# Three seven-product units per chunk of the gate and up projections, in place of two, with the sums of weights and the closing sums reordered

## What is computed

```python
def swiglu(x, w_gate, w_up, w_down):
    return (jax.nn.silu(x @ w_gate) * (x @ w_up)) @ w_down
h = h + 0.5 * swiglu(rms_norm(h, ffn1_norm[l]), ffn1_w_gate[l], ffn1_w_up[l], ffn1_w_down[l])
```

## Time and profile before

| | before |
|---|---|
| time, median of 3 runs | 1835.81 us |
| profiled execution: first to last instruction | 1834.2 us |
| PE busy | 99% |
| DVE busy | 82% |
| ACT busy | 54% |
| DMA | 380.36 MB, mean 207 GB/s |
| mean granted TensorE clock | 0.999 |

### The profile page before, as it was taken

The page is one execution under the profiler, slowest core; times in us unless marked ns, Lnnn a source line. Parts: engine busy times, 40 slices in busy tenths (PEclk is TensorE's granted clock), DMA queues, the critical chain, the costliest instruction groups (busy, mean ns, idle before and its releaser), DMA issues. The chain is left out here.

```text
span 1834.2 us, 29749 instructions
## 1 busy us (share of the span) xinstructions
PE 1819.6 (99%) x10696; PEld 1546.4 (84%) x10696; DVE 1505.4 (82%) x1755; ACT 995.2 (54%) x1181; POOL 11.1 (1%) x23
## 2 busy tenths in 40 slices
PE   9999999999999999999999999999999999999998
PEld 7888888888888888999998878888888888888886
DVE  5888888888988985788867866688888888889996
ACT  7555555545555655754535655545555555555554
POOL 1000000000000000000000000000000000000000
PEclk9999999999999999999999999999999999999999
DMA  7677666777766778564443557677777677676664
GB/s 252 221 219 228 219 216 215 220 229 236 233 202 204 225 224 267 173 184 140 138 116 106 176 171 261 180 232 231 229 224 232 216 227 222 217 240 195 209 208 157
DMA packets 207851, 380.36 MB, mean 207 GB/s; under 512 B 16016, under 2 KB 35728, under 8 KB 207504
## 3 DMA queue, kind: packets, MB, share of 16 engines
q1 hardware_dynamic: 206768, 377.08, 65.7%
q10 hardware_dynamic: 480, 1.97, 0.3%
q0 software_dynamic: 512, 0.06, 0.0%
HBM read 360.19 MB, written 18.87 MB: 207 GB/s over the span
## 5 line engine op out<-in xcount | busy, mean ns | idle before, releaser
L402 ACT CAST whi<-raw 128x1024 fp32r<-128x1024 f32 (+1 forms) x648 | 675.1, 1047 | 700.8 <-DVE raw L1476 189.6
L411 DVE TENSOR_TENSOR wlo<-raw,whi 128x1024 fp32r<-128x1024 f32 (+1 forms) x648 | 771.7, 1212 | 208.4 <-ACT whi L402 194.5
L428 PE MATMUL psA<-whi,xh 128*128 128x512 f32 (+1 forms) x572 | 219.5, 384 | 0.5 <-DVE wlo L411 0.5
L428 PE MATMUL psA<-whi,xl 128*128 128x512 f32 (+1 forms) x572 | 219.2, 383 | 0.0
L428 PE MATMUL psA<-wlo,xh 128*128 128x512 f32 (+1 forms) x572 | 219.1, 383 | 0.0
L428 PE MATMUL psB<-whi,xh 128*128 128x512 f32 x544 | 211.7, 389 | 0.0
L428 PE MATMUL psB<-wlo,xh 128*128 128x512 f32 x544 | 211.6, 389 | 0.0
L428 PE MATMUL psB<-whi,xl 128*128 128x512 f32 x544 | 211.6, 389 | 0.0
L428 PEld LDWEIGHTS psA<-whi,xh 128*128 128x128 f32 x572 | 107.4, 188 | 21.6 <-DVE wlo L411 0.7
L428 PEld LDWEIGHTS psA<-whi,xl 128*128 128x128 f32 x572 | 107.4, 188 | 21.2
L428 PEld LDWEIGHTS psA<-wlo,xh 128*128 128x128 f32 x572 | 107.4, 188 | 21.0
(11 more groups left out here) (520 smaller groups left out, 3447.3 us busy)
## 6 DMA issues: line engine op xcount, KB each, us to landing
raw<-in_ffn_w_gate SPq DMA_DIRECT2D x176, 512.0 KB, 4.5
raw<-in_ffn_w_up SPq DMA_DIRECT2D x176, 512.0 KB, 4.6
raw<-in_ffn_w_down SPq DMA_DIRECT2D x176, 512.0 KB, 4.6
raw<-in_w_in SPq DMA_DIRECT2D x80, 512.0 KB, 3.6
raw<-in_w_out SPq DMA_DIRECT2D x32, 512.0 KB, 4.2
quads_dram<-stage SPq DMA_DIRECT2D x88, 128.0 KB, 4.2
stage<-quads_dram SPq DMA_DIRECT2D x22, 512.0 KB, 4.3
x<-in_x SPq DMA_DIRECT2D x4, 512.0 KB, 7.5
```

Source lines behind the costliest of these rows:

```text
L402: nc.scalar.copy(whi[:, slot, :, 0:ncol], raw[:, slot, :, 0:ncol]).then_inc(hi_ready, 1)
L411: nc.vector.tensor_tensor(wlo[:, slot, :, 0:ncol], raw[:, slot, :, 0:ncol], whi[:, slot, :, 0:ncol].bitcast(F32), ALU.subtract).then_inc(l ...
L428: mm = nc.tensor.matmul(ps[:, tb, 0:ncol], lhs[:, k0 + t, tok], rhs[:, slot, t, 0:ncol], start=(first and t == 0 and p == 0 and tb != open ...
```

## The change

A chunk has three units (pairs 2, 3 and 4) and ten plain groups: gate 0, 1, 5, 6; unit 0; gate 7, up 0; unit 1; up 1, up 5; unit 2; up 6, 7. Two plain groups lie between any two units and behind the last.

The sums of weights for a unit are three instructions, not four (up's two rows; less gate's first row; then two rows at once, the second rows of both groups less that difference), with signs turned where they are closed. The gate group's low part goes in front of the last two of them, and the group is reported ready by the last. The high parts of the sums are made in two instructions, of which the second waits for it. `close_gate` moves from group 14 to 15 and no longer waits for the last unit in front of its sum on the even half of `psA`; `turned_hi` and `turned_lo` move to group 3 of the next chunk. Chunk 0 takes the up groups in another order, so that pairs 2 to 4 are used first. Some tiles are placed anew in memory. The same sums serve the down stage.

```diff
-GATE_UNITS = 2
+GATE_UNITS = 3
 GATE_PAIR = 2
-CHUNK = ([("gate", j) for j in (0, 1, 4, 5)] + [("unit", 0)] + [("gate", j) for j in (6, 7)] + [("up", 0)] + [("unit", 1)]
-         + [("up", j) for j in (1, 4, 5, 6, 7)])
+CHUNK = ([("gate", j) for j in (0, 1, 5, 6)] + [("unit", 0)] + [("gate", 7), ("up", 0)] + [("unit", 1)]
+         + [("up", 1), ("up", 5)] + [("unit", 2)] + [("up", j) for j in (6, 7)])
+FIRST_UP = list(range(GATE_PAIR, GATE_PAIR + GATE_UNITS))
+FIRST_UP += [j for j in range(GD) if j not in FIRST_UP]
...
-        def split_lo(base, n, per, j, ncol=COLS):
+        def split_lo(base, n, per, j, ncol=COLS, read_on=False):
...
+            low = nc.vector.tensor_tensor(wlo[:, slot, :, 0:ncol], raw[:, slot, :, 0:ncol],
+                                          whi[:, slot, :, 0:ncol].bitcast(F32), ALU.subtract)
+            if not read_on:
+                low.then_inc(lo_ready, 1)
...
-            product(Q6, *token_sums(0), *column_sums(1), first, last)
-            product(Q5, *tokens(0, 1), *column_sums(0), first, last)
-            product(psA[:, 1, :], *tokens(1, 1), *column_sums(2), False, last).then_inc(unit_used, 1)
+            gate_row, up_row = pair_rows(gate, up)
+            product(Q6, *token_sums(0), *column_sums(0), first, last)
+            product(Q5, *tokens(0, 1), *column_sums(up_row), first, last)
+            product(psA[:, 1, :], *tokens(1, 1), *column_sums(gate_row), False, last).then_inc(unit_used, 1)
...
@@ ffn_load @@
-                        if g == 13:
+                        if g == PER - 2:
                             quads_load(sp, f, n - 1)
...
@@ ffn_act, chunk @@
-                        nc.scalar.wait_ge(col_step, n * (4 * GATE_UNITS) + (4 * unit + 2))
+                        nc.scalar.wait_ge(col_step, n * (2 * GATE_UNITS) + (2 * unit + 1))
                         split_hi(base, n, PER, g + 1)
-                        unit_hi(n, unit)
-                    if g == PER - 2:
+                        unit_hi(base, n, PER, g, unit)
+                    if g == SLOTS - 1 and not (isinstance(n, int) and n == 1):
+                        turned_hi(n - 2)
+                    if g == PER - 1:
 
                         nc.scalar.wait_ge(quads_stored, n * 64 + 64 * f * FC)
-                        nc.scalar.wait_ge(unit_used, n * GATE_UNITS + FIRST_UNIT[f])
+                        nc.scalar.wait_ge(group_used, n * PER + (base + last_gate + 1))
                         nc.scalar.copy(silu[:, 0, :], Q1).then_inc(share_copied, 1)
                 silu_gate(n)
-                turned_hi(n - 1)
...
@@ unit_hi @@
-            nc.scalar.copy(col_hi[:, :, :], col_sum[:, :, :]).then_inc(col_hi_ready, 1)
+            nc.scalar.wait_ge(col_step, n * (2 * GATE_UNITS) + (2 * unit + 2))
+            nc.scalar.copy(col_hi[:, 0, :], col_sum[:, 0, :])
+            nc.scalar.wait_ge(lo_ready, n * per + base + g + 1)
+            nc.scalar.copy(col_hi[:, 1:3, :], col_sum[:, 1:3, :]).then_inc(col_hi_ready, 1)
...
@@ unit_sums @@
+            tt(raw[:, up, 0, :], raw[:, up, 0, :], raw[:, up, 1, :], ALU.add).then_inc(col_step, 1)
+            split_lo(base, n, per, g, read_on=True)
...
-            tt(col_sum[:, 0, :], raw[:, gate, 0, :], raw[:, up, 0, :], ALU.add).then_inc(col_step, 1)
-            nc.vector.wait_ge(col_step, steps + (4 * unit + 1))
-            tt(raw[:, up, 0, :], raw[:, up, 0, :], raw[:, up, 1, :], ALU.add).then_inc(col_step, 1)
-            tt(col_sum[:, 1, :], col_sum[:, 0, :], raw[:, up, 1, :], ALU.add).then_inc(col_step, 1)
-            nc.vector.wait_ge(col_step, steps + (4 * unit + 3))
-            tt(col_sum[:, 2, :], col_sum[:, 1, :], raw[:, gate, 1, :], ALU.add).then_inc(col_step, 1)
+            nc.vector.wait_ge(col_step, steps + (2 * unit + 1))
+            tt(col_sum[:, 0, :], raw[:, up, 0, :], raw[:, gate, 0, :], ALU.subtract).then_inc(col_step, 1)
+            nc.vector.wait_ge(col_step, steps + (2 * unit + 2))
+            tt(col_sum[:, 1:3, :], raw[:, low:high + 1:high - low, 1, :],
+               col_sum[:, 0, :].unsqueeze(1).to_broadcast([P, 2, COLS]), ALU.subtract).then_inc(lo_ready, 1)
+            split_lo(base, n, per, g + 1)
...
@@ close_gate @@
-                tt(shares[:, 0, :], Q6, silu[:, 0, :], ALU.subtract).then_inc(closed, 1)
                 tt(psA[:, 0, :], psA[:, 0, :], silu[:, 0, :], ALU.add)
+                nc.vector.wait_ge(unit_used, n * GATE_UNITS + FIRST_UNIT[f])
+                tt(shares[:, 0, :], Q6, silu[:, 0, :], ALU.add).then_inc(closed, 1)
...
@@ first_chunk (DVE) @@
-                        nc.vector.wait_ge(group_used, base + GD + GATE_PAIR + GATE_UNITS)
+                        nc.vector.wait_ge(group_used, base + GD + GATE_UNITS)
...
@@ ffn_dve, chunk @@
-                        split_lo(base, n, PER, g)
-                        split_lo(base, n, PER, g + 1)
                         unit_lo(n, unit)
...
-                    if g == 1 and not (isinstance(n, int) and n == 1):
-                        turned_lo(n - 2)
                     if g == SLOTS - 1:
+                        if not (isinstance(n, int) and n == 1):
+                            turned_lo(n - 2)
                         gate_up(n - 1)
-                    if g == PER - 2:
+                    if g == PER - 1:
                         close_gate(n)
...
@@ ffn_dve, down @@
-                if i == 1:
+                if i == SLOTS - 1:
                     turned_lo(FC - 2)
-                if i == SLOTS - 1:
                     gate_up(FC - 1)
```

More of the change, by code:

```diff
@@ L80 @@
 CONST_WIDTH = 2816
+BEYOND = 256
 def down_order(f, m):
@@ L191, in build @@
         to_channels = consts[:, 1792:2816].rearrange("p (t c) -> p t c", c=P)
+        token_scale = sb("token_scale", [P, S])
+        same_r = sb("same_r", [P, P], F32R)
+        sb("beyond_consts", [P, BEYOND])
         prow = sb("prow", [P, P])
@@ L291, in build @@
         hl_sum = at("hl_sum", [P, KF, S], arena, plus=KF * S * 4)
-        token_scale = sb("token_scale", [P, S])
-        same_r = sb("same_r", [P, P], F32R)
         widx_scale = sb("widx_scale", [P, TB])
@@ L410, in split_lo @@
                 nc.vector.wait_ge(group_used, n * per + g - SLOTS + 1)
-            nc.vector.tensor_tensor(wlo[:, slot, :, 0:ncol], raw[:, slot, :, 0:ncol],
-                                    whi[:, slot, :, 0:ncol].bitcast(F32), ALU.subtract).then_inc(lo_ready, 1)
+            low = nc.vector.tensor_tensor(wlo[:, slot, :, 0:ncol], raw[:, slot, :, 0:ncol],
+                                          whi[:, slot, :, 0:ncol].bitcast(F32), ALU.subtract)
+            if not read_on:
+                low.then_inc(lo_ready, 1)
         def wait_group(base, n, per, j):
@@ L431, in project_tokens, with pair_rows @@
             mm.then_inc(group_used, 1)
+        def pair_rows(gate, up):
+            return (1, 2) if gate < up else (2, 1)
         def unit_products(base, n, per, g, whole, pair, sums, j, unit, first, last):
@@ L676, in chunk @@
                         xq_load(sp, 2, 2)
-                for j in range(GD):
-                    load_group(sp, rows(w_up, j * KT)[:, :, 0:COLS], base, 0, PER, GD + j)
+                for i, j in enumerate(FIRST_UP):
+                    load_group(sp, rows(w_up, j * KT)[:, :, 0:COLS], base, 0, PER, GD + i)
             chunk(0)
@@ L732, in first_chunk @@
                         halves_hi(xh, xl_sum, x_sum_hi, x_sum, GATE_PAIR // 2, sum_number(f))
+            last_gate = max(g for kind, j, g in chunk_items() if kind == "unit")
             def chunk(n):
@@ L758, in ffn_act @@
                 if kind == "unit":
-                    nc.scalar.wait_ge(col_step, 4 * unit + 2)
+                    nc.scalar.wait_ge(col_step, 2 * unit + 1)
                     split_hi(down, 0, 0, g + 1)
-                    unit_hi(0, unit, col_raw)
+                    unit_hi(down, 0, 0, g, unit, col_raw)
                     unit += 1
+                if i == SLOTS - 1:
+                    turned_hi(FC - 2)
                 if i == GD + SLOTS:
@@ L777, in ffn_act, with unit_hi @@
                 squares_act(3, 2)
-        def unit_hi(n, unit, col_sum=col_sum):
-            nc.scalar.wait_ge(col_step, n * (4 * GATE_UNITS) + (4 * unit + 4))
+        def unit_hi(base, n, per, g, unit, col_sum=col_sum):
             if not (isinstance(n, int) and n * GATE_UNITS + unit == 0):
                 nc.scalar.wait_ge(unit_used, n * GATE_UNITS + unit)
-            nc.scalar.copy(col_hi[:, :, :], col_sum[:, :, :]).then_inc(col_hi_ready, 1)
+            nc.scalar.wait_ge(col_step, n * (2 * GATE_UNITS) + (2 * unit + 2))
+            nc.scalar.copy(col_hi[:, 0, :], col_sum[:, 0, :])
+            nc.scalar.wait_ge(lo_ready, n * per + base + g + 1)
+            nc.scalar.copy(col_hi[:, 1:3, :], col_sum[:, 1:3, :]).then_inc(col_hi_ready, 1)
         def unit_sums(base, n, per, g, unit, col_sum=col_sum):
             gate, up = (base + g) % SLOTS, (base + g + 1) % SLOTS
-            steps = n * (4 * GATE_UNITS)
```

(25 more changed lines are left out.)

## The result

The changed kernel took 1850.65 us (median of 4 runs, 1849.07 to 1853.51), the kernel before 1835.82: ratio 1.0083, interval 1.0071 to 1.0094. It is slower by 14.8 us, where 10.5 had been forecast. The profiled execution is the slowest of the four, with a span of 1851.7 us.

What follows compares the result with a forecast made beforehand. PE, without a gap in a chunk, was taken to bound the kernel. -13.6 + 13.8 + 10.3 = +10.5 us on the span of 1834.2 gave 1844.7, so a median of 1846.3 us; range for 8 in 10: 1833 to 1855.

Steps and rivals of the forecast that it cites:

- The saving: Gate and up chunks: a third unit replaces two plain groups, 21 matmuls for 24, in 20 chunks: 13.6 us less.
- DVE's sums: Unit sums on DVE: 6.4 us per unit for 6.6, two-row sum 1.22; 3.8 us more DVE work per chunk.
- The end of a chunk: Behind the last unit: PE stands still 0.69 us at each of 20 chunk ends, 13.8 us.
- The chain: Last unit, closing sums, silu, next chunk's first high and low part: ready at T + 6.13, PE wants it at T + 5.44.
- The lower bound of 0.55: Least chunk-end stall, in us, if DVE hears of PE at the modelled end and nothing is lost on taking up.
- 1.1 us early: DVE before the closing sums at a chunk's end: claimed ready this long before PE, with unit 2 starting at S + 26.2.
- idle time before its reader: SP's queue: the turned quads' load moves one group, with many us idle before its reader; counted at nothing.
- (d): Slower still: DVE waits 2 us for loads at two units per chunk, closing sums start late; 1864 us, chance 0.10.
- The start of a chunk: DVE's queue up to group 6: PE loses 0.57 us by then in 18 chunks, 10.3 us.
- (a): Faster: the chain at the chunk's end is covered and the full saving stays; 1822.2 us, chance 0.13.
- (b): Same: stall at chunk ends, but DVE catches up before unit 0, none at group 6; 1836.0 us, chance 0.17.
- (c): The forecast itself, stalls at chunk ends and starts outweighing the saving: 1839.5 to 1854 us, chance 0.60.

Runs made afterwards that it cites:

- early_and_late: Changed kernel with the next chunk's first high part before silu on ACT and the turned quads' load behind group 15: 1823.20 us, 0.9925 of before.
- late_quads_load: Changed kernel with SP's load of the turned quads behind group 15 of a chunk, not behind groups 12 and 13: 1844.57 us, 1.0044 of before.
- turn_later: Changed kernel with DVE's block transpose of the last chunk's product behind group 6's low part, not in front: 1850.50 us, in a later set 1842.51.
- changed_5: The changed kernel as it is, run again in the third set on the first set's chip: 1848.14 us.
- early_high: Changed kernel with the high part of the next chunk's first group in front of silu on ACT: 1831.23 us, 0.9973 of before.
- early_late_later: Changed kernel with first high part before silu, turned quads' load behind group 15 and transpose behind group 6's low part: 1823.12 us, 0.9934 of before.

## Why the prediction held, point by point

- **The saving, -13.6 us:** as counted. early_and_late has no gaps and a span 12.7 us below before's. Its 20 chunks took 13.3 us less (829.9 for 843.2), and what lies outside them took 0.6 more. A chunk of 183 matmuls took 41.48 us, 0.2267 us each again, and not the 0.216 that the Trainium skill gives in "TensorE: Matmul & The Clock Gate", section "Wait — 56ns, not 53.3ns?".
- **DVE's sums:** the two-row sum took 1.22 to 1.23 us, as taken. DVE's work per chunk rose by 3.7 us. The prediction wrote 3.8; its own terms, 6.4 - 2.3 - 2 x 0.2, give 3.7.
- **The end of a chunk, +13.8 us forecast, 19.6 in the profile.** The chain was right step by step; where DVE is ready in time it is 0.69 us (late_quads_load). The lower bound of 0.55 does not follow from its two conditions, which take 0.10 each off 0.69; nothing came near it. The error is the start of the chain: the prediction had DVE "1.1 us early". It used 4.14 us for unit 2's second load, from one row, though the page of before gives a median of 4.6 for that kind, and held the move of the quads' load to cost nothing, naming "idle time before its reader". Its reader had time; the unit's load beside it had not. That is the step that failed, rival (d) in a mild form: a load of 6 us in place of 4.1. With the quads' load moved back it was 4.9, so more than half of the 1.8 us is the move and the rest the one row taken for all.
- **The start of a chunk, +10.3 us forecast, 5.3 in the profile.** Place and mechanism were right: late at group 6, moved away by turn_later, and a little at unit 0's last products (0.03 us per chunk for 0.24). It was mis-sized, 0.29 us per chunk for 0.57, or 0.35 with the starts that the table leaves out. Most of that is the hand-overs: between DVE's two-row sum, ACT's cast and DVE's next row they are 0.04 and 0.02 us (195.83 to 195.87, 196.93 to 196.95), where I took 0.12 each.
- **Unit 2, nothing forecast, 3.5 us in the profile,** by the same load.
- **Luck.** The errors offset each other in part, -5.0 against +5.8 and +3.5. The sum was made for the profiled span, and there it missed by 7.0 us (1844.7 for 1851.7), in the slowest of the four runs; it came within 4.3 us of the median, and within 2 us of that of changed_5. That closeness is partly luck. The sign is not, since the chain alone equals the saving.
- **Rivals.** (a) and (b) fall: stalls at every chunk end and at group 6. (c) is what happened, with (d)'s cause added to it.

## What to carry over

An edit that saves work on the fullest engine can take away the cover of the loop's tail: write down the chain from its last product to the next pass's first input in program order, with every queue that it passes, and compare it with the matmuls left behind it. Here it was 6.1 us over 5.4, and one instruction on ACT, moved in front of silu, together with the quads' load moved behind two more weight loads, turned a loss of 12.5 us (changed_5) into a gain of 12.5. A transfer put in "idle" time can compete with the one issued just before it; look at who waits for that one.

## Not expected

- A 512 KB load issued 0.5 us behind another can lengthen the earlier one: 5.96 us to its reader in one chunk, against 4.87 when the next one came 2.9 us later. The medians from issue to landing are 5.9 us in the first profile of the changed kernel and 5.8 in early_high, 4.9 with the quads' load late in both. It does not always do so: in changed_5 the median is 5.2, between 4.7 and 6.3, at the same distance of 0.53 us, and what decides it was not found. DVE's waits for it scatter from 0.6 to 2.5 us within that profile. The changed kernel's runs scatter too (1845.9 to 1853.5 in two sets of runs), while early_late_later, where PE never waits for it in the end, stays within 1823.1 and 1824.3.
- When PE takes up work after a wait, the second matmul comes 0.34 us behind the first (228.13 to 228.47), at pace 0.23: each late group costs 0.11 us more than its lateness, 2 us of the 30 at chunk starts alone.
